# A sparse attention's index scores in a new order, and a third tile for scores in five attentions

## The reference

```python
c_q = rms_norm(c_q); c_kv = rms_norm(c_kv)                # 256 and 128 features
q     = einsum('btr,rhd->bthd', c_q, w_uq)                 # 8 heads of 64
q_lat = einsum('bthd,hdc->bthc', q, w_uk)                  # latent queries, 128 features
q_idx = einsum('btr,rhd->bthd', c_q, w_qi)                 # index queries
# per block of 128 queries:
score = einsum('bth,bths->bts', w_idx, relu(einsum('bthd,bsd->bths', q_idx, k_idx)))
score = where(key_pos <= q_pos, score, -inf)
top_val, top_idx = top_k(score, 64)                        # 64 of 256 keys
s = einsum('bthc,btkc->bthk', q_lat, c_kv[top_idx]) * 64**-0.5
o = einsum(softmax(s), c_kv[top_idx])
```

## Time and profile before

| | |
|---|---|
| median of 3 runs | 2186.6 us (2179.37 to 2188.9) |
| the profiled execution | 2185.26 us, its span 2183.5 us |
| busy | TensorE 2058.9 us (94%), VectorE 1392.1 (64%), ScalarE 945.8 (43%), GpSimd 31.9 (1%) |
| mean granted clock | 0.969 |
| HBM | 156 GB/s over the span |

### The profile page before, as it was taken

The page is one execution under the profiler, slowest core; times in us unless marked ns, Lnnn a source line. Parts: engine busy times, 40 slices in busy tenths (PEclk is TensorE's granted clock), DMA queues, the critical chain, the costliest instruction groups (busy, mean ns, idle before and its releaser), DMA issues. The chain is left out here.

```text
span 2183.5 us, 37138 instructions
## 1 busy us (share of the span) xinstructions
PE 2058.9 (94%) x15066; PEld 1910.8 (88%) x15066; DVE 1392.1 (64%) x1849; ACT 945.8 (43%) x1258; POOL 31.9 (1%) x48
## 2 busy tenths in 40 slices
PE   6989999999989999999998989999999994899998
PEld 6869988999869988998997878998899894788997
DVE  6757756655657765774667555775577456565773
ACT  4454434333444444444344343444444432544442
POOL 0000000000000000000000010000000000000000
PEclk9999999999999999999999789999999997999999
DMA  7325554343324554555530133455455552142553
GB/s 284 134 100 193 189 206 171 147 167 133 148 75 167 192 202 157 191 191 202 195 126 1 59 110 142 156 190 204 157 190 193 201 188 96 49 154 94 187 201 116
DMA packets 49788, 341.46 MB, mean 156 GB/s; under 512 B 5776, under 2 KB 6544, under 8 KB 9616
## 3 DMA queue, kind: packets, MB, share of 16 engines
q1 hardware_dynamic: 45216, 321.21, 40.5%
q10 hardware_dynamic: 4464, 18.68, 2.3%
HBM read 338.82 MB, written 1.05 MB: 156 GB/s over the span
## 5 line engine op out<-in xcount | busy, mean ns | idle before, releaser
L304 DVE TENSOR_TENSOR wlo<-raw,whi 128x2048 fp32r<-128x2048 f32 x288 | 659.9, 2291 | 307.6 <-ACT whi L297 306.8
L228 PE MATMUL pj<-xh,whi 128*128 128x256 f32 x2704 | 761.9, 282 | 19.0 <-DVE wlo L314 13.8
L229 PE MATMUL pj<-xl,whi 128*128 128x256 f32 x2704 | 759.9, 281 | 0.0
L230 PE MATMUL pj<-xh,wlo 128*128 128x256 f32 x2704 | 757.8, 280 | 0.0
L297 ACT ACTIVATE whi<-raw 128x2048 fp32r<-128x2048 f32 x299 | 569.3, 1910 | 420.8 <-PE acc L236 198.7
L228 PEld LDWEIGHTS pj<-xh,whi 128*128 128x128 f32 x2704 | 512.2, 189 | 22.1 <-issue 16.3
L229 PEld LDWEIGHTS pj<-xl,whi 128*128 128x128 f32 x2704 | 511.5, 189 | 0.1
L230 PEld LDWEIGHTS pj<-xh,wlo 128*128 128x128 f32 x2704 | 509.9, 189 | 0.0
L234 PE MATMUL acc<-whi,AR 128*128 128x512 f32 x656 | 257.8, 393 | 6.7 <-DVE AR L1967 4.4
L235 PE MATMUL acc<-whi,AR 128*128 128x512 f32 x656 | 256.7, 391 | 0.0
L236 PE MATMUL acc<-wlo,AR 128*128 128x512 f32 x656 | 256.5, 391 | 0.0
(11 more groups left out here) (351 smaller groups left out, 2424.9 us busy)
## 6 DMA issues: line engine op xcount, KB each, us to landing
raw<-in_wstream SPq DMA_DIRECT2D x302, 1024.0 KB, 4.8
F<-in_gains ACTq DMA_DIRECT2D x12, 512.0 KB, 4.4
F<-in_rpb ACTq DMA_DIRECT2D x3, 1024.0 KB, 4.8
F<-in_memtok ACTq DMA_DIRECT2D x2, 1024.0 KB, 4.7
F<-in_memin ACTq DMA_DIRECT2D x2, 1024.0 KB, 6.9
F<-in_small ACTq DMA_DIRECT2D x1, 1536.0 KB, 10.2
F<-in_xin SPq DMA_DIRECT2D x2, 512.0 KB, 7.3
xt<-in_xtok SPq DMA_DIRECT2D x1, 1024.0 KB, 11.9
```

The costliest lines, as they stand in the source:

```text
L228: nc.tensor.matmul(o, wh, k_hi, start=first, stop=False, skip_group_check=True)
L229: nc.tensor.matmul(o, wh, k_lo, start=False, stop=False, skip_group_check=True)
L230: return nc.tensor.matmul(o, wl, k_hi, start=False, stop=last, skip_group_check=True)
L304: nc.vector.tensor_tensor(wlo[:, gs, :], raw[:, gs, :], whi[:, gs, :].bitcast(F32), ALU.subtract).then_inc(w_lo, 1)
```

## The change

In the sparse stage TensorE projects the index queries first, then turns the keys, makes all logits, and only then projects with UQ and makes the latent queries; ScalarE's copies follow this order. The first half of the queries is scored against, and selected from, its 128 possible keys only (`NK`). VectorE starts the convolution and does its first block before it waits for CQ's factors. In all five attentions the score tiles become three (`S`, chosen by u modulo their number), and softmax_a waits for the transposes of unit u-3; the tiles of the copied transposes stay two. Lines that only say "..." stand for what is left out.

```diff
--- before.py
+++ after.py
@@ -595,11 +595,16 @@
+        def score_tile(u, U):
+            return U["S"][u % len(U["S"])]
...
+            S = score_tile(u, U)
             if "slots" not in U:
-                return [(acc[2 + u % 2], Sb[:, u % 2, 0:U["nk"]], PTb[:, u % 2, 0:U["nk"]])]
-            S, PT = U["slots"][u % 2]
+                return [(acc[2 + u % 2], S, PTb[:, u % 2, 0:U["nk"]])]
+            PT = U["slots"][u % 2]
@@ -607,7 +612,7 @@
             n = U["nk"] // U["H"]
-            S = U["slots"][u % 2][0] if "slots" in U else Sb[:, u % 2, :]
+            S = score_tile(u, U)
@@ -645,7 +650,7 @@
                     pe.wait_ge(*at(tag, "od", U["per"] * (U["grp"] + 1 - deep)))
-                PT = U["slots"][u % 2][1] if "slots" in U else PTb[:, u % 2, :]
+                PT = U["slots"][u % 2] if "slots" in U else PTb[:, u % 2, :]
@@ -668,15 +673,15 @@
                 dve.wait_ge(*at(tag, "s", u + 1))
-                if u >= 2:
-                    dve.wait_ge(*at(tag, "pt", n_parts(U) * (u - 1)))
+                back = len(U["S"])
+                if u >= back:
+                    dve.wait_ge(*at(tag, "pt", n_parts(U) * (u + 1 - back)))
...
                 link(dve, x)
-                S = U["slots"][u % 2][0] if "slots" in U else Sb[:, u % 2, 0:U["nk"]]
-                nc.vector.tensor_reduce(sm[:, H * (u % 2):H * (u % 2) + H], S.rearrange("p (a n) -> p a n", a=H), AXX,
+                nc.vector.tensor_reduce(sm[:, H * (u % 2):H * (u % 2) + H], score_tile(u, U).rearrange("p (a n) -> p a n", a=H), AXX,
@@ -738,11 +743,12 @@
-        def two_heads(q, k, v_, soft, t, grp, n_idle):
+        def two_heads(q, k, v_, soft, t, grp, n_idle, third):
...
                         nk=2 * T, H=2, soft=[soft(t)] * 2, grp=grp, per=2, end=t == 1, idle=n_idle,
+                        S=(Sb[:, 0, :], Sb[:, 1, :], third),
@@ -895,10 +901,11 @@
                 MK = take(64)
+                S3 = take(512)
...
                 DM = take(2, 512)
-                slots = [(Sb[:, :, :].rearrange("p a n -> p (a n)"), PTb[:, :, :].rearrange("p a n -> p (a n)")),
-                         (take(1024), take(1024))]
+                slots = [PTb[:, :, :].rearrange("p a n -> p (a n)"), take(1024)]
+                SS = (Sb[:, :, :].rearrange("p a n -> p (a n)"), take(1024), take(1024))
@@ -932,7 +939,8 @@
                         S, ps, HD ** -0.5, b, ALU.mult, ALU.add) for a in range(2)]
-                    out_.append(dict(scores=sc, pv=pv, nk=2 * T, H=2, soft=soft, grp=grp, per=1, end=t == 1))
+                    out_.append(dict(scores=sc, pv=pv, nk=2 * T, H=2, soft=soft, grp=grp, per=1, end=t == 1,
+                                     S=(Sb[:, 0, :], Sb[:, 1, :], S3)))
@@ -949,7 +957,7 @@
                     out_.append(dict(scores=sc, pv=pv, nk=1024, H=2, soft=soft, grp=grp, per=1, end=t == 1,
-                                     slots=slots))
+                                     slots=slots, S=SS))
@@ -1104,12 +1112,13 @@
             V = take(2, XH * P)
+            S3 = take(512)
...
                                lambda t: lambda S, ps: nc.vector.tensor_scalar(S, ps, P ** -0.5, None, ALU.mult), t, g,
-                               3)
+                               3, S3)
@@ -1207,8 +1217,10 @@
                                lambda t: lambda s_, ps: nc.vector.scalar_tensor_tensor(
-                                   s_, ps, 64 ** -0.5, MBs[:, t, :], ALU.mult, ALU.add), t, g, 1)
+                                   s_, ps, 64 ** -0.5, MBs[:, t, :], ALU.mult, ALU.add), t, g, 1, S3)
                      for g in range(DH // 2) for t in range(2)]
+            NK = (P, T)
@@ -1241,16 +1253,29 @@
                 pe.wait_ge(S("ld"), 32)
-                for W, banks in ((UQ, (acc[1], acc[2])), (QIw, (acc[3], pj[0]))):
+                def queries(W, banks):
...
                     last.then_inc(S("q"), 1)
+                queries(QIw, (acc[3], pj[0]))
...
                 last.then_inc(S("q"), 1)
+                for v_ in range(8):
+                    t, a = divmod(v_, 4)
+                    if v_ < 2:
+                        pe.wait_ge(S("qc"), 2 + v_)
+                    else:
+                        pe.wait_ge(S("relu"), v_ - 1)
+                    for odd in range(2):
+                        rows = slice(64 * odd, 64 * odd + 64)
+                        last = nc.tensor.matmul(lbank(v_, odd)[:, 0:NK[t]], QI[rows, a, t * P:(t + 1) * P],
+                                                CK[rows, 0:NK[t]], start=True, stop=True)
+                    last.then_inc(S("lg"), 1)
+                queries(UQ, (acc[1], acc[2]))
@@ -1259,15 +1284,6 @@
                 last.then_inc(S("ql"), 1)
-                for v_ in range(8):
-                    t, a = divmod(v_, 4)
-                    if v_ >= 2:
-                        pe.wait_ge(S("relu"), v_ - 1)
-                    for odd in range(2):
-                        rows = slice(64 * odd, 64 * odd + 64)
-                        last = nc.tensor.matmul(lbank(v_, odd), QI[rows, a, t * P:(t + 1) * P], CK[rows, :],
-                                                start=True, stop=True)
-                    last.then_inc(S("lg"), 1)
@@ -1305,33 +1321,38 @@
                     .then_inc(S("mv"), 1)
+                def conv(k):
+                    y = hb[:, k, :]
+                    link(dve, nc.vector.tensor_scalar(y, U[:, k, 0:T], v("cw0", k), v("cb", k), ALU.mult, ALU.add))
+                    link(dve, nc.vector.scalar_tensor_tensor(y, U[:, k, 1:T + 1], v("cw1", k), y, ALU.mult, ALU.add))
+                    link(dve, nc.vector.scalar_tensor_tensor(y, U[:, k, 2:T + 2], v("cw2", k), y, ALU.mult, ALU.add))
+                    nc.vector.tensor_tensor(y, y, bb[:, k, :], ALU.mult).then_inc(S("cv"), 1)
+                nc.vector.memset(SC[:, 0, P:T], 0.0)
+                nc.vector.memset(U[:, :, 0:2], 0.0)
+                link(dve, nc.vector.tensor_tensor(U[:, :, 2:T + 2], cb_, hb, ALU.mult))
+                conv(0)
...
-                nc.vector.memset(U[:, :, 0:2], 0.0)
-                link(dve, nc.vector.tensor_tensor(U[:, :, 2:T + 2], cb_, hb, ALU.mult))
                 dve.wait_ge(S("cn"), 3)
-                for k in range(4):
-                    y = hb[:, k, :]
-                    link(dve, nc.vector.tensor_scalar(y, U[:, k, 0:T], v("cw0", k), v("cb", k), ALU.mult, ALU.add))
-                    link(dve, nc.vector.scalar_tensor_tensor(y, U[:, k, 1:T + 1], v("cw1", k), y, ALU.mult, ALU.add))
-                    link(dve, nc.vector.scalar_tensor_tensor(y, U[:, k, 2:T + 2], v("cw2", k), y, ALU.mult, ALU.add))
-                    nc.vector.tensor_tensor(y, y, bb[:, k, :], ALU.mult).then_inc(S("cv"), 1)
+                for k in range(1, 4):
+                    conv(k)
...
                         h = 2 * a + odd
+                        sc_, rl = SC[:, t, 0:NK[t]], RL[:, v_ % 2, odd, 0:NK[t]]
                         if h == 0:
-                            x = nc.vector.tensor_scalar(SC[:, t, :], RL[:, 0, 0, :] if v_ % 2 == 0 else RL[:, 1, 0, :],
-                                                        WI[:, t, 0:1], None, ALU.mult)
+                            x = nc.vector.tensor_scalar(sc_, rl, WI[:, t, 0:1], None, ALU.mult)
                         else:
-                            x = nc.vector.scalar_tensor_tensor(SC[:, t, :], RL[:, v_ % 2, odd, :], WI[:, t, h:h + 1],
-                                                               SC[:, t, :], ALU.mult, ALU.add)
+                            x = nc.vector.scalar_tensor_tensor(sc_, rl, WI[:, t, h:h + 1], sc_, ALU.mult, ALU.add)
@@ -1341,9 +1362,9 @@
                     for t in range(2):
-                        link(dve, nc.vector.max(M8[:, t, :], SC[:, t, :]))
+                        link(dve, nc.vector.max(M8[:, t, :], SC[:, t, 0:NK[t]]))
                     for t in range(2):
-                        link(dve, nc.vector.match_replace(SC[:, t, :], M8[:, t, :], SC[:, t, :], -3e38))
+                        link(dve, nc.vector.match_replace(SC[:, t, 0:NK[t]], M8[:, t, :], SC[:, t, 0:NK[t]], -3e38))
@@ -1363,21 +1384,29 @@
                             nc.scalar.activation(C2[:, k, :], CQ[:, k, :], ACT.Square).then_inc(S("sq"), 1)
-                act.wait_ge(S("q"), 3)
-                for d, bank in ((QT[:, 0:2], acc[1]), (QT[:, 2:4], acc[2]), (QI[:, 0:2], acc[3]), (QI[:, 2:4], pj[0])):
+                def copy_q(d, bank):
                     nc.scalar.activation(d.rearrange("p a t -> p (a t)"), bank[:, :], ACT.Copy).then_inc(S("qc"), 1)
-                nc.scalar.activation(CT.rearrange("p a t -> p (a t)"), mb[:, 0:T], ACT.Copy).then_inc(S("qc"), 1)
-                act.wait_ge(S("ql"), 1)
-                for b in range(4):
-                    nc.scalar.activation(QL[:, 2 * b:2 * b + 2, :].rearrange("p a t -> p (a t)"), acc[b][:, :],
-                                         ACT.Copy).then_inc(S("qlc"), 1)
+                act.wait_ge(S("q"), 1)
```

(14 more changed lines are left out.)

## The result

The changed kernel takes 2158.85 us, the median of 4 runs (2156.41 to 2163.88); the kernel before took 2187.75 on the same chip (4 runs). The ratio is 0.9881 (0.9856 to 0.9906): faster, as forecast, by 28.9 us where the forecast had 24.1; 2162.5 was forecast, with a range of 2154 to 2172. The profiled execution took 2156.41 us with a span of 2154.6, against 2185.26 and 2183.5 before.

The account below looks back on a forecast made before the run. TensorE was taken as the bound, with shorter work helping in most stages and order only where it stands still. Terms 9.6 - 0.1 + 3.2 + 3.5 + 2.5 + 4.7 + 0.7 = 24.1 us gave 2162.5 against the median, range 2154 to 2172.

Parts of the forecast that it names:

- part 1: Sparse stage: index queries and logits before the latent branch let VectorE's score sums start 9.6 us earlier (9 to 10).
- part 2: Sparse stage: 128 keys for the first 128 queries save 0.133 us on each of 24 VectorE operations, 3.2 us (0 to 5).
- part 3: Sparse attention: a third score tile cuts a unit from 3.02 to 2.68 us, 3.5 us in all (2.5 to 4).
- part 4: Neighbourhood attention: a third score tile shortens VectorE's waits for transposes, 2.5 us (1.5 to 3).
- part 5: Dilated attention: a third score tile gains 1.1 us at each of two weight stalls and 2.5 in the tail, 4.7 together.
- part 6: Two memory attentions: with a third score tile waits of 0.20 and 0.17 go, 0.7 us for both (0.4 to 1).
- 4.0 + 6 x 0.19 + 0.2 to drain: Sparse stage, TensorE's 16 index-query matmuls: 10 in the first 4 us at 1.2 GHz, six at 2.4 GHz, ending at 1821.4.
- CQ does not move: Sparse stage: VectorE's work ahead of its wait fits the 3.25 us gap, 0 to 0.3 us late, 0.1 taken.
- What is queued behind: Sparse stage: UQ's projection starts at about 1828, the latent branch ends by 1837.6 to 1844.2, mask due at 1846.5.
- The rival in which it comes after the mask: Sparse stage: the latent branch, all at 1.2 GHz, ends after the mask; 2164.5 us if 4 us more; chance 0.04.
- The rival of TensorE at half clock: Slower than before: half clock lasts through sparse attention and output projection, costing up to 46 us, about 2208; chance 0.02.
- I give the tail 0.3: Neighbourhood attention behind TensorE's 5.08 us stall: TensorE busy almost throughout, so an estimated 0.3 us gain there.

Follow-up runs that it names:

- the old order: Changed kernel with the sparse attention's previous order, latent products before index scores and convolution after normalisation, keeping three score tiles and 128 keys: 2163.83 us.
- all 256 keys: Changed kernel with 256 keys for both halves of the queries and the memset of the unused half gone: 2168.16 us, one run.
- two tiles: Changed kernel with two score tiles used in turn in all five attentions, index order and 128-wide first half kept: 2172.97 us.
- the late convolution: Changed kernel with VectorE's gated product and first convolution block put back behind the normalisation of CQ: 2159.95 us, one run.
- the three edits: Changed kernel with 8-column matmuls interleaved, product and first convolution block after the normalisation, first index logits waiting for the first query copy only: 2154.68 us.
- VectorE held back: Changed kernel with VectorE waiting for GpSimd's power, all four convolution blocks after the normalisation, first logits waiting for one query copy: 2152.17 us.

## Why the prediction was right

The profiled executions differ by 28.9 us of span. Where a run or a second trace separates a term from the clock it is measured apart; what code that is the same in both traces took less is named as clock.

| step of the prediction | forecast | measured | from |
|---|---|---|---|
| part 1, index scores first | 9.5 | 7.8 | 8.85 earlier start, less 1.07 of GpSimd; 8.4 by the old order |
| part 2, half as many keys | 3.2 | 3.1 | all 256 keys |
| part 3, third tile, sparse attention | 3.5 | 3.6 | 28.82 to 25.19 |
| part 4, neighbourhood | 2.5 | 3.6 | before against after, 0.5 of it the clock (below) |
| part 5, dilated | 4.7 | 5.0 | against two tiles, same time at half clock |
| part 6, memory, two | 0.7 | 1.75 | 0.84 and 0.91 |
| not forecast: clock | 0 | 3.6 | dilated 2.0, projection of the sparse stage 1.6 |

The rows add up to 28.45; the remaining 0.4 is the shorter first stage of that execution.

The sum is nearer than its terms: part 1 fell 1.7 us short, parts 4 to 6 gave more than forecast, and these misses cancel. That much of the agreement is luck.

**Part 1** lost 1.7 us at two places. The step "4.0 + 6 x 0.19 + 0.2 to drain", for the 16 matmuls of the index queries, had the clock rise 4 us after TensorE began; it rose after 5.3, and the queries took 6.33 us instead of 5.4. And the step "CQ does not move", "0 to 0.3 us late", priced VectorE's new work before the wait at its own duration and found room for it; it did fit (it ends at 1801.2, the wait at 1802.3), but it ran beside GpSimd's power, which is on the path and took 1.07 longer. That it did so because of VectorE the two runs show in which VectorE has at most a memset of 0.17 us during the power (1.02 and 1.01), and the run with all 256 keys, where the product begins 0.15 us earlier and the power is 0.14 shorter. The Trainium skill (GPSIMD Engine Reference, Specifications) says that GpSimd shares its SBUF interfaces with VectorE, and that the two meet where a VectorE instruction has two SBUF inputs (or runs in a two-port mode). The product has two, and this trace agrees: 2.08 us for 1.01.

The two places go together in all twelve profiles. In the six in which the power took 1.01 us (before and five runs) the query matmuls start 4.5 to 4.6 us after the start of the power, the clock is back at 1.00 at 7.4 to 8.3, and the first 16 take 5.1 to 5.6 us. In the six in which it took 1.94 to 2.08 they start at 5.4 to 5.6, the clock is back at 10.8 to 11.7, and they take 6.3 to 6.7. So TensorE's start, 1.1 us late, went each time with queries at least 0.7 us longer; why the clock answers so is not shown. The forecast of 5.4 was right for the start that it assumed. I read the moved work for TensorE and VectorE and left out the third engine that was at work just then. So the attention's first scores came 10.9 us earlier after the statistics and not the 12.7 named as a sign.

**Part 2** was right to 0.1: the slope of the 256 to 512 product holds for MAX8, MATCH_REPLACE8 and the sums at 128, 133 ns each. The fixed part of an operation is paid at either width, and the elements are saved. The formula of the Trainium skill (VectorE: DVE Perf Modes, the section on the TRN2 errata) gives 291 ns at 128, an estimate; MAX8 took 295 and MATCH_REPLACE8 274. Its rule to tile at 512 elements or more, read as a threshold, did not hold here.

**What is queued behind** was right in place and off in size: UQ begins 4.4 us after the first sum, as in the forecast (1828 against 1823.7), but the clock stayed at 1.00, so that the branch ends 8.3 us before the mask and not 2. The rival in which it comes after the mask was further away than it was priced. The rival of TensorE at half clock, the slower side, did not appear either: the clock did fall while TensorE waited for the mask, and the first four score matmuls took 2.04 us, as they had in before, 2.05.

**Part 3** came out as its steps say: 2.63 per unit for 2.68. Its terms add up to 3.36 and not to the 3.5 written there; measured were 3.6.

**Part 4** had the stall before scores 12 right (4.28 for "some 4.3"), and the time up to it: 2.46 us of gain for 2.2. The step that was mis-sized is "I give the tail 0.3": between scores 12 and the output projection 22.79 us for 23.83, so 1.04. Half of it is not the tile's. From scores 12 to scores 13 it took 5.44 us for 5.98, and the clock was down for 4.6 us of the one and 5.8 of the other; with two tiles again it was 6.11 with 6.1. Scores 13 to 14 and 14 to 15 took 3.4 each in all three. Left are 0.5 us at the end, where TensorE's two idle times of 0.28 and 0.18 before transposes became one of 0.18. So the tail is worth 0.5 for 0.3.

**Part 5**: the weight stalls are 0.55 for 1.65 and 2.11 for 3.55, 1.1 and 1.44 less, where 1.1 each was forecast, and the tail from scores 13 to the output projection gave 2.55 (24.88 us for 27.43) for 2.5. A first reading, that a shorter stall also spares the stage its half clock, did not hold: with two tiles and the long stalls the stage had 13.7 us at half clock, with three 13.7 in two executions and 6.8 in the third.

**Part 6** was mis-sized: "the waits of 0.20 and 0.17 go" took the profile's idle time, which counts from the drained end of a matmul. From transposes to transposes the two middle units went from 2.97 and 3.02 to 2.59 and 2.63 us, 0.38 and 0.39 less. Part 3 did this sum start to start and came out right; part 6 took the idle time of its row.

**The total**: over its three sets of runs the kernel after had ratios of 0.9881, 0.9855 and 0.9861, 29 to 35 us below before. The parts, without what is named as clock in the table and in part 4, make 24.3. The rest goes with less time at half clock in the traces (137 us before; 119, 103 and 99 after), but why the shorter kernel meets less of it isn't settled; there was one trace of before.

## What to carry to other kernels

Before work is moved into a gap of one engine, look at what every other engine does in that gap: the gap was real here, and the work slowed the engine that made it. A late start of TensorE can cost more than itself, since the clock may come back later too. Read waits that recur in a pipeline from start to start and not from the drained end. Cutting a row of VectorE operations from 256 to 128 elements is worth its elements, and a branch that the next stage needs only later belongs behind the one that it waits for first. Where the clock moves unchanged code by more than the candidate's gain, compare stages between marks, not totals.

## What the runs showed of the hardware that was not expected

- GpSimd's power on 128x4 took 1.01 us alone, 2.08 with a 128x1024 fp32 product of VectorE (1.21 us) that began with it, 1.94 when that product had begun 0.15 us earlier, and 1.01 again when VectorE waited.
- After TensorE's wait for that power the clock came back 7.4 to 8.3 us after its start where TensorE's queries began at 4.5 to 4.6 us, and 10.8 to 11.7 us after it where they began at 5.4 to 5.6 (six profiles each).
- The granted clock fell to 0.50 in a stretch of unbroken matmuls, with a row of 8-column matmuls before it and without one; the same code took 51.98 to 53.59 us by it, and the stretch with the mixer 401.7 to 408.5.
- While TensorE waited for the mask the clock was down (0.50), yet through the logits, with TensorE busy 59% to 89% of a window in short pairs, it stayed at 1.00, where before it had fallen to 0.68 in such a stretch. In the three runs whose sums start earlier (the late convolution, the three edits, VectorE held back) it fell to 0.50 again amid the logits, for 3.4 us, so the new order by itself does not keep it up.
